# Interleaving two weight slots per row tile, an earlier square root for the key norms, and V transposes between the output gate's groups

## The chip, the cores and the metric

The kernel runs on one core of one Trainium2 chip. The metric is device time of one launch in microseconds (us). Before the change it is 1481.89 us, the median of three runs (1480.38 to 1483.07).

## What is computed

One inference step of a two-layer decoder, on 16 meta rows and 256 prompt rows of a new sequence and 8 new rows of each of 8 running sequences: 336 rows of 1024 columns, later 322 or 320, since some rows are needed no longer. Cut to what matters:

```python
def _swiglu(x, w_gu, w_down):
    gate, up = jnp.split(x @ w_gu, 2, axis=-1)
    return (jax.nn.silu(gate) * up) @ w_down

# layer 0 (RWKV-7 time mix), layer 1 (short convolution)
x = x + 0.5 * _swiglu(_rmsnorm(x, n_a), w_gu_a, w_down_a)
x = x + mixer(_rmsnorm(x, n_m))
x = x + 0.5 * _swiglu(_rmsnorm(x, n_b), w_gu_b, w_down_b)

# in the time mix, h is the normed x, xx the shifted h minus h
xr, xw, xk, xv, xa, xg = [h + xx * mu[c] for c in range(6)]
k = xk @ w_rkv[1]; v = xv @ w_rkv[2]
kk = k * k_k, divided by its norm in each head of 64
g = sigmoid(xg @ g1) @ g2
S = S * d + (S @ -kk) b + v k        # for each step in time; y = S @ r
out = ((groupnorm(y) + bonus) * g) @ w_o
```

A final RMSNorm ends the step; the states of the mixers are outputs too.

## The kernel before

Every matmul with weights is done with 32-bit values split in a high and a low part, in three passes: `(w_hi, x_hi)`, `(w_hi, x_lo)`, `(w_lo, x_hi)`. Activations lie transposed: 128 columns of the model on the partitions, 336 rows of the sequence along the free axis, so x is eight tiles, k = 0 to 7. A **slot** is 16 weight tiles of 128x128 (1 MB): two output tiles for all eight k, 48 matmuls of 336, 322 or 320 columns.

There are two slot buffers, even and odd. For every slot SyncE loads `w_raw`, ScalarE makes `w_hi` (L243, in `split_act`) when TensorE has used the slot before last, VectorE makes `w_lo` (L248, in `split_dve`), and TensorE waits for that (`lo_ready`, in `pe_slot_wait`). So from the end of one slot to the start of the slot two further on there lie one `w_hi`, one `w_lo`, and whatever stands ahead of them on ScalarE and VectorE. In a steady stretch the slot in between covers this.

The stages in order: FFN 0 (`ffn_pe`, `ffn_dve` with its inner `gu_slot`, ScalarE's side at L383 and L385; weights `in_gu`, then `in_down`), the time mix, the projection `wo`, FFN 1, FFN 2, the input projection of the convolution, the projection `scout`, FFN 3, the final norm. Each engine has its program written out by hand, and semaphores link them; so what stands behind a waiting instruction on its engine waits as well.

- An FFN's first slot (slot 0) runs while x_hi (L307) and x_lo (L295) arrive one tile at a time; TensorE waits for each tile (L330, in `pe_pair`). Slot 1 follows, the sum of squares (L311) stands between them. ScalarE first splits slot 2, then makes 1/rms by a logarithm and an exponential (`norm_act`, L315 and L317), VectorE scales the two results of slot 0 (L422, L423) and then makes `w_lo` of slot 2.
- The time mix begins with the key projection: slots 0 to 3 of `in_mix` with the mixed tiles x_hi (L1117) and x_lo (L1375), each slot run whole (L804). Later the sum of squares of every key head is turned into its inverse norm: VectorE's maximum, ScalarE's Sqrt (L1206), VectorE's reciprocal (L1437), TensorE's spreading over a head's partitions (L852). Sqrt stands between two of four groups of sigmoids on ScalarE (L1131).
- After the V projection TensorE runs the output gate as four groups of two output tiles (`lora_out`, L830), then turns V of the first two chunks (`turn_v`, L958; ScalarE copies the result to `uvs`, L1275), does the first `couple_v` (L967), then `state_rows` (L1032): 256 small matmuls that multiply the states of the eight running sequences with their rows. The chain over the chunks follows (from L983).
- `wo` and `scout` (`project_pe`, L498) take four slots from o_hi and o_lo. Slot 2 writes the PSUM banks of slot 0, so it waits for `x_new`: VectorE's L275, which adds a result to x, for both output tiles of slot 0. Between these two, VectorE's program has the split of slot 2.

Of the kernel before, what the change touches and what calls it, by code (L numbers as in the profile page):

```python
# [77 lines left out]
def build_program(nc, x_dram, vec_dram, const_dram, shift_dram, conv_dram, wkv_dram, gu_dram, down_dram,  # L78
                  mix_dram, wo_dram, scin_dram, scout_dram, blockeye_dram, y_out, wkvp_out, wkvs_out, shift_out,
                  convo_out, zt_dram, tt_dram):  # L80
    with ExitStack() as ctx:
# [330 lines left out]
        def ffn_dve(dve, f):  # L412
# [4 lines left out]
            def gu_slot(i, par, tiles, first=False):  # L417
                s = 2 * i + par
                if first:
                    norm_dve(dve, {0: 0, 1: 2, 2: 3, 3: 5}[f], n)  # L420
# [61 lines left out]
        def project_pe(pe, name, q, n, olo_base):  # L482

            first = stream[name][0]
            for s in range(4):
                pe_slot_wait(pe, first + s)
                pe.wait_ge(x_new, 8 * q + 2 * s - 2)
                if s == 0:
                    pe.wait_ge(scaled, SCALED_BEFORE[name])
                    if name == "wo":  # L490
                        pe.wait_ge(mix_evac, MIX_GROUPS - 4)
                banks = ((2 * s) % 4, (2 * s + 1) % 4)
                for k in range(KT):
                    if s == 0:
                        pe.wait_ge(olo_ready, olo_base + k + 1)
                    for j in range(2):
                        for i, (w, v) in enumerate(passes(whi[s % 2], wlo[s % 2], ohi, olo)):
                            last = pe.matmul(PS[:, banks[j], :n], w[:, (2 * k + j) * P:(2 * k + j + 1) * P], v[:, k, :n],  # L498
                                             start=(k == 0 and i == 0), stop=(k == KT - 1 and i == 2))
# [270 lines left out]
        def mix_pe(pe):  # L770
# [167 lines left out]
        def chain_pe(pe):  # L938
# [7 lines left out]
            def turn_v(i):  # L946
# [3 lines left out]
                else:  # L950
                    pe.wait_ge(vy_padded, 1)
                    pe.wait_ge(mix_evac, 21)
# [149 lines left out]
        def mix_act(act):  # L1102
# [140 lines left out]
            for s in range(4):  # L1243
                evac(GATE_GROUP + s, [(gate[:, m, :], ACT.Copy, None, False) for m in (2 * s, 2 * s + 1)])
            split(17)
            chain_act(act)
# [528 lines left out]
```

## Time and profile before

| | |
|---|---|
| median of three runs | 1481.89 us |
| profiled execution | 1481.93 us |
| its span, first to last instruction | 1480.1 us |
| TensorE busy | 1402.2 us, 95% |
| VectorE busy | 853.8 us, 58% |
| ScalarE busy | 584.7 us, 40% |
| mean granted TensorE clock | 0.965 |

The profiled execution is 0.04 us from the median. Times of rows are microseconds from the start of the span; a row of the timeline has start, duration, engine (PE is TensorE, PEld its weight load, DVE VectorE, ACT ScalarE, POOL GpSimd), line, operation, tiles, and in brackets how long the engine stood idle before it and what released it. TensorE's matmuls overlap: the distance of their starts tells the pace, not their durations. The granted clock is 1.00 at 2.4 GHz and 0.50 at 1.2 GHz.

### The profile page before, as it was taken

What the parts mean: (1) busy time and instruction counts of PE and PEld (TensorE: products, weight loads), DVE (VectorE), ACT (ScalarE), POOL (GpSimd) and SP (SyncE); (2) the same over time, 40 slices, a digit from 0 to 9 for tenths busy, and PEclk for the clock granted to TensorE, in tenths of its full rate; (3) what the DMA queues carried; (4) which work ended last, traced back from release to release, by engine and by line L of the source; (5) the groups of instructions that cost most, each with busy time, mean ns of one, the idle gap of its engine ahead of it and who ended that gap; (6) DMA issues with size and microseconds to landing.
All of it is one profiled execution on the core that took longest, in us unless ns stands there. A gap on an engine that the chain in (4) does not pass through costs nothing.

```text
span 1480.1 us, 28445 instructions
## 1 busy us (share of the span) xinstructions
PE 1402.2 (95%) x11742; PEld 1359.1 (92%) x11742; DVE 853.8 (58%) x1275; ACT 584.7 (40%) x754; POOL 22.8 (2%) x36
## 2 busy tenths in 40 slices
PE   4999999697799999899999999999999999999997
PEld 4999999586689996699999999999999999999997
DVE  4555544776868254665555455555546766555543
ACT  5333333476344331354333334433333235433332
POOL 0000000300000000200000000000000000000000
PEclk9999999898799797799999999999999999999999
DMA  4433334232135111034433444443444444434342
GB/s 193 151 140 138 137 131 155 86 116 85 60 84 187 36 48 53 29 131 154 142 142 126 147 162 150 154 142 124 139 157 149 147 143 140 167 143 142 128 155 96
DMA packets 44219, 188.97 MB, mean 128 GB/s; under 512 B 15888, under 2 KB 17296, under 8 KB 28016
## 3 DMA queue, kind: packets, MB, share of 16 engines
q1 hardware_dynamic: 44144, 187.89, 36.9%
q8 instruction: 57, 0.93, 0.3%
q14 instruction: 18, 0.15, 0.0%
HBM read 182.65 MB, written 5.22 MB: 127 GB/s over the span
## 4 chain that ended last, share of the span: by engine, by line
PE 87%; DVE 5%; ACT 4%; issue 2%; POOL 1%; DMA 1%; SPq 0%; ACTq 0%; DVEq 0%
PE psum L330 46%; PE psum L362 21%; PE psum L804 5%; PE psum L498 4%; ACT w_hi L243 2%; PE psum L1032 1%; DVE w_lo L248 1%; PE psum L983 1%; PE psum L1052 1%; PE psum L830 1%; PE psum L1001 1%; PE psum L958 1%; PE psum L876 1%; DMA w_raw<-in_gu 1%; PE psum L1048 1%
## 5 line engine op out<-in xcount | busy, mean ns | idle before, releaser
L330 PE MATMUL psum<-x_hi,w_hi 128*128 128x322 f32 (+2 forms) x1600 | 501.4, 313 | 23.5 <-DVE x_lo L295 17.8
L248 DVE TENSOR_TENSOR w_lo<-w_raw,w_hi 128x2048 fp32r<-128x2048 f32 (+1 forms) x188 | 388.2, 2065 | 226.3 <-ACT w_hi L243 225.9
L243 ACT ACTIVATE w_hi<-w_raw 128x2048 fp32r<-128x2048 f32 (+1 forms) x188 | 325.8, 1733 | 459.3 <-PE psum L330 227.2
L330 PE MATMUL psum<-x_lo,w_hi 128*128 128x322 f32 (+2 forms) x1600 | 500.8, 313 | 0.0
L330 PE MATMUL psum<-x_hi,w_lo 128*128 128x322 f32 (+2 forms) x1600 | 499.4, 312 | 0.0
L330 PEld LDWEIGHTS psum<-x_hi,w_hi 128*128 128x128 f32 x1600 | 302.2, 189 | 26.4 <-issue 22.7
L330 PEld LDWEIGHTS psum<-x_hi,w_lo 128*128 128x128 f32 x1600 | 302.9, 189 | 0.0
L330 PEld LDWEIGHTS psum<-x_lo,w_hi 128*128 128x128 f32 x1600 | 302.7, 189 | 0.3
L362 PE MATMUL psum<-h_hi,w_hi 128*128 128x322 f32 (+2 forms) x704 | 219.5, 312 | 0.0
L362 PE MATMUL psum<-h_lo,w_hi 128*128 128x322 f32 (+2 forms) x704 | 219.4, 312 | 0.0
L362 PE MATMUL psum<-h_hi,w_lo 128*128 128x322 f32 (+2 forms) x704 | 219.2, 311 | 0.0
L362 PEld LDWEIGHTS psum<-h_hi,w_hi 128*128 128x128 f32 x704 | 132.8, 189 | 0.0
L362 PEld LDWEIGHTS psum<-h_hi,w_lo 128*128 128x128 f32 x704 | 132.8, 189 | 0.0
L362 PEld LDWEIGHTS psum<-h_lo,w_hi 128*128 128x128 f32 x704 | 132.5, 188 | 0.0
L385 ACT ACTIVATE h_hi<-tmp 128x322 f32 (+5 forms) x88 | 41.9, 476 | 210.6 <-DVE tmp L427 210.6
L422 DVE TENSOR_TENSOR tmp<-psum,rstd 128x322 f32<-128x322 f32 (+2 forms) x88 | 43.7, 497 | 131.1 <-PE psum L330 106.7
L804 PE MATMUL psum<-x_hi,w_hi 128*128 128x336 f32 x208 | 70.0, 337 | 11.2 <-DVE x_lo L1375 11.2
L429 DVE TENSOR_TENSOR h_lo<-tmp,h_hi 128x322 f32 (+5 forms) x88 | 43.9, 498 | 63.8 <-ACT h_hi L385 63.8
L804 PE MATMUL psum<-x_lo,w_hi 128*128 128x336 f32 x208 | 68.5, 329 | 0.0
L804 PE MATMUL psum<-x_hi,w_lo 128*128 128x336 f32 x208 | 68.2, 328 | 0.0
L275 DVE SCALAR_TENSOR_TENSOR x<-psum,x 128x322 f32<-128x322 f32 (+5 forms) x48 | 23.7, 494 | 72.6 <-PE psum L362 62.4
L804 PEld LDWEIGHTS psum<-x_hi,w_hi 128*128 128x128 f32 x208 | 41.3, 198 | 16.1 <-issue 12.8
(200 smaller groups left out, 1394.2 us busy)
## 6 DMA issues: line engine op xcount, KB each, us to landing
w_raw<-in_gu SPq DMA_DIRECT2D x88, 1024.0 KB, 4.7
w_raw<-in_down SPq DMA_DIRECT2D x64, 704.0 KB, 4.1
w_raw<-in_mix SPq DMA_DIRECT2D x16, 1024.0 KB, 4.7
w_raw<-in_scin SPq DMA_DIRECT2D x12, 1024.0 KB, 4.8
w_raw<-in_wo SPq DMA_DIRECT2D x4, 1024.0 KB, 5.5
w_raw<-in_scout SPq DMA_DIRECT2D x4, 1024.0 KB, 4.7
s<-in_wkv SPq DMA_DIRECT2D x8, 256.0 KB, 3.4
out_wkvs<-s SPq DMA_DIRECT2D x8, 256.0 KB, 2.0
```

The source lines that it names most:

```text
L243: act.activation(whi[par][:, :tiles * P], raw[par][:, :tiles * P], ACT.Copy).then_inc(hi_ready, 1)
L248: dve.tensor_tensor(wlo[par][:, :n], raw[par][:, :n], whi[par][:, :n].bitcast(F32), ALU.subtract).then_inc(lo_ready, 1)
L275: dve.scalar_tensor_tensor(out=x[:, m, c:], in0=ps[:, :T - c], scalar=alpha, in1=x[:, m, c:], op0=ALU.mult, op1=ALU.add).then_inc(x_new, 1)
L330: last = pe.matmul(PS[:, banks[j], :n], w[:, (2 * k + j) * P:(2 * k + j + 1) * P], v[:, k, :n], start=(k == 0 and i == 0), stop=(k == KT - ...
L362: last = pe.matmul(PS[:, 4 + par, :n], w[:, k * P:(k + 1) * P], v[:, kk, :n], start=(kk == 0 and i == 0), stop=(kk == FT - 1 and i == 2))
L385: act.activation(hhi[:, bass.ds(s, 1), :n], tmp[3][:, :n], ACT.Copy).then_inc(hhi_ready, 1)
L422: dve.tensor_tensor(tmp[0][:, :n], PS[:, 2 * par, :n], rstd[:, :n], ALU.mult).then_inc(gate_scaled, 1)
L429: dve.tensor_tensor(hlo[:, bass.ds(s, 1), :n], tmp[3][:, :n], hhi[:, bass.ds(s, 1), :n].bitcast(F32), ALU.subtract).then_inc(hlo_ready, 1)
L498: last = pe.matmul(PS[:, banks[j], :n], w[:, (2 * k + j) * P:(2 * k + j + 1) * P], v[:, k, :n], start=(k == 0 and i == 0), stop=(k == KT - ...
L804: last = pe.matmul(PS[:, b + j, shift:shift + T], w[:, (2 * k + j) * P:(2 * k + j + 1) * P], v[:, k, :], start=(k == 0 and i == 0), stop=( ...
L830: last = pe.matmul(PS[:, b + j, shift:shift + T], w[:, tile * P:(tile + 1) * P], v[:, k, :], start=(n == 0 and i == 0), stop=(n == len(inn ...
L876: last = pe.matmul(PS[rows, 2 + c // 8, (c % 8) * HD:(c % 8 + 1) * HD], bk[rows, p, c, :, :].rearrange("p h t -> p (h t)"), con[rows, K_EY ...
```

## The change

Seven edits, by the lines of the new kernel where they are named so:

1. **FFN 0, front.** A generator `dual(lag)` yields tiles of slot 0 and slot 1 in turn, slot 1 `lag` tiles behind; `pe_tile` runs the six matmuls of one tile of one slot. FFN 0 uses a lag of 2; slot 0's last tile is then the 13th of 16 before the sum of squares (which now stands ahead of slot 1's last two tiles).
2. **`norm_act`.** Ahead of the wait for the sum of squares, for the time mix's norm and the final norm, one Ln of one column into a new tile `spare`.
3. **FFN `gu_slot` on VectorE.** For the first slot, the split of slot 2 stands ahead of the wait for 1/rms and of the scaling.
4. **Key projection.** Slots 0 and 1 in turn, with a lag of 3.
5. **Key norms.** VectorE's maximum and ScalarE's Sqrt stand before the first group of decay sigmoids, VectorE's reciprocal between the tiles of the receptance input.
6. **Output gate and V.** Gate group, `turn_v(0)`, two gate groups, `turn_v(1)`, gate group; the gate's PSUM banks change from (4, 6, 0, 2) to (4, 0, 2, 4), ScalarE's evacuations follow the same order, its split of the slot after (`split(17)`) goes behind them, and the semaphore values are fitted to it.
7. **`wo` and `scout`.** TensorE waits for both slots 0 and 1, then runs them in turn with a lag of 3; slots 2 and 3 as before.

```diff
+        def dual(lag):
+
+            for step in range(KT + lag):
+                if step < KT:
+                    yield 0, step
+                if step >= lag:
+                    yield 1, step - lag
...
-            gu_slot(0, 0, fresh=True)
-            norm_pe(pe, {0: 0, 1: 2, 2: 3, 3: 5}[f], 0, n)
-            gu_slot(0, 1)
+            if f == 0:
+                pe_slot_wait(pe, gu)
+                pe.wait_ge(scaled, d["scaled"] + 2)
+                for par, k in dual(2):
+                    if par == 0:
+                        pe.wait_ge(xlo_ready, 8 * d["ver"] + k + 1)
+                    elif k == 0:
+                        pe_slot_wait(pe, gu + 1)
+                    elif k == KT - 2:
+                        norm_pe(pe, 0, 0, n)
+                    last = pe_tile(pe, par, (2 * par, 2 * par + 1), k, n, xhi, xlo)
+                    if k == KT - 1:
+                        last.then_inc(slot_used, 1)
...
         def norm_act(act, norm, n):
+            if norm in (1, 6):
+                act.activation(spare[:, 0:1], con[:, K_ONES:K_ONES + 1], ACT.Ln)
...
                 if first:
+                    split_dve(dve, gu // 2 + i + 1, par, tiles)
                     norm_dve(dve, {0: 0, 1: 2, 2: 3, 3: 5}[f], n)
...
-                split_dve(dve, gu // 2 + i + 1, par, tiles)
+                if not first:
+                    split_dve(dve, gu // 2 + i + 1, par, tiles)
...
         def project_pe(pe, name, q, n, olo_base):
...
+            for s in range(2):
                 pe_slot_wait(pe, first + s)
                 pe.wait_ge(x_new, 8 * q + 2 * s - 2)
+            for s, k in dual(3):
                 if s == 0:
+                    pe.wait_ge(olo_ready, olo_base + k + 1)
+                last = pe_tile(pe, s, (2 * s, 2 * s + 1), k, n, ohi, olo)
...
-            for s in range(4):
-                project(s, XK, s == 0, s == 3, PAD)
+            pe_slot_wait(pe, MIXB)
+            banks = [open_group(), open_group()]
+            for par, k in dual(3):
...
+            for s in range(2, 4):
+                project(s, XK, False, s == 3, PAD)
...
+            act.wait_ge(kk_max, 1)
+            act.activation(tmp[3][0:HEADS, :T], tmp[3][0:HEADS, :T], ACT.Sqrt).then_inc(kk_root, 1)
             for s in range(4):
                 x_hi_tile(XR, 2 + s)
...
                 factors(s)
-                if s == 1:
-                    act.wait_ge(kk_max, 1)
-                    act.activation(tmp[3][0:HEADS, :T], tmp[3][0:HEADS, :T], ACT.Sqrt).then_inc(kk_root, 1)
...
                 low(XR, k)
                 if k == 1:
                     lora_low(1, 1)
...
+                if k == 3:
+                    dve.wait_ge(kk_root, 1)
+                    dve.reciprocal(rstd[0:HEADS, :], tmp[3][0:HEADS, :T]).then_inc(kk_inv, 1)
             split(6)
-            dve.wait_ge(kk_root, 1)
-            dve.reciprocal(rstd[0:HEADS, :], tmp[3][0:HEADS, :T]).then_inc(kk_inv, 1)
...
+            gate_group(0)
             turn_v(0)
+            gate_group(2)
+            gate_group(4)
             turn_v(1)
-            pe.wait_ge(mix_evac, 22)
+            gate_group(6)
+            pe.wait_ge(v_turned, 1)
+            pe.wait_ge(mix_evac, 21)
...
+            take_gate(0)
             take_v(0)
+            take_gate(1)
+            take_gate(2)
             take_v(1)
+            take_gate(3)
+            split(17)
```

How it moves instructions, at three places. First VectorE's program where FFN 0 begins its first pair of weight columns, right after the last x_lo (it reads the same in FFN 1 to 3). Before:

```order
L422 TENSOR_TENSOR tmp_62<-psum,rstd 128x336 [waits slot_used,rstd_ready]
L423 TENSOR_TENSOR tmp_64<-psum,rstd 128x336
L248 TENSOR_TENSOR w_lo_54<-w_raw_50,w_hi_52 128x2048 [waits hi_ready]
L427 TENSOR_TENSOR tmp_65<-tmp_63,tmp_64 128x336 [waits scaled,act_ready]
L429 TENSOR_TENSOR h_lo<-tmp_65,h_hi 128x336 [waits hhi_ready]
```

Now:

```order
L249 TENSOR_TENSOR w_lo_54<-w_raw_50,w_hi_52 128x2048 [waits hi_ready]
L455 TENSOR_TENSOR tmp_63<-psum,rstd 128x336 [waits slot_used,rstd_ready]
L456 TENSOR_TENSOR tmp_65<-psum,rstd 128x336
L461 TENSOR_TENSOR tmp_66<-tmp_64,tmp_65 128x336 [waits scaled,act_ready]
L463 TENSOR_TENSOR h_lo<-tmp_66,h_hi 128x336 [waits hhi_ready]
```

The split of slot 2 has moved ahead of the two scalings, and so ahead of their wait for `rstd_ready`.

Next TensorE's program in `scout`, around the fourth tile of slot 0 (`w_hi_52` and `w_lo_54` are the even buffer's, `w_hi_53` and `w_lo_55` the odd one's). Before:

```order
L498 MATMUL psum<-o_hi,w_hi_52 128x320 [waits olo_ready]
L498 MATMUL psum<-o_lo,w_hi_52 128x320
L498 MATMUL psum<-o_hi,w_lo_54 128x320
L498 MATMUL psum<-o_hi,w_hi_52 128x320
L498 MATMUL psum<-o_lo,w_hi_52 128x320
L498 MATMUL psum<-o_hi,w_lo_54 128x320
L498 MATMUL psum<-o_hi,w_hi_52 128x320 [waits olo_ready]
```

Now, in the same place:

```order
L349 MATMUL psum<-o_hi,w_lo_54 128x320
L349 MATMUL psum<-o_hi,w_hi_53 128x320
L349 MATMUL psum<-o_lo,w_hi_53 128x320
L349 MATMUL psum<-o_hi,w_lo_55 128x320
L349 MATMUL psum<-o_hi,w_hi_53 128x320
L349 MATMUL psum<-o_lo,w_hi_53 128x320
L349 MATMUL psum<-o_hi,w_lo_55 128x320
L349 MATMUL psum<-o_hi,w_hi_52 128x320 [waits olo_ready]
```

and at the end of slot 0, with the first row of slot 2 at the end:

```order
L349 MATMUL psum<-o_lo,w_hi_52 128x320
L349 MATMUL psum<-o_hi,w_lo_54 128x320
L349 MATMUL psum<-o_hi,w_hi_53 128x320
L349 MATMUL psum<-o_lo,w_hi_53 128x320
...
L349 MATMUL psum<-o_hi,w_lo_55 128x320
L349 MATMUL psum<-o_hi,w_hi_52 128x320 [waits x_new,lo_ready]
```

Before, the even buffer's slot ran on to its end and the odd one's 48 matmuls followed; now tiles take turns from the fourth on, and between slot 0's last matmul and slot 2's first there stand 24 matmuls. FFN 0 and the key projection have the same pattern, with lags of 2 and 3.

Last TensorE's program from the gate's groups to `state_rows`. Before:

```order
L830 MATMUL psum<-t_hi,w_lo_55 128x336
L958 MATMUL psum<-con,vy 64x64 [waits mix_evac,vy_padded]
L958 MATMUL psum<-con,vy 64x64 x15
L958 MATMUL psum<-con,vy 64x64 [waits v_turned]
L958 MATMUL psum<-con,vy 64x64 x15
L967 MATMUL psum<-uvs_102,z 32x64 [waits mix_evac]
L967 MATMUL psum<-uvs_102,z 32x64 x15
L1032 MATMUL psum<-ar,s_0_112 64x2x8 [waits mix_evac,s0_loaded0]
```

Now:

```order
L867 MATMUL psum<-t_hi,w_lo_55 128x336
L1005 MATMUL psum<-con,vy 64x64 [waits z_ready,mix_evac,vy_padded]
L1005 MATMUL psum<-con,vy 64x64 x15
L867 MATMUL psum<-t_hi,w_hi_53 128x336 [waits mix_evac]
...
L867 MATMUL psum<-t_hi,w_lo_55 128x336
L1005 MATMUL psum<-con,vy 64x64 [waits v_turned]
L1005 MATMUL psum<-con,vy 64x64 x15
L867 MATMUL psum<-t_hi,w_hi_53 128x336 [waits mix_evac]
...
L867 MATMUL psum<-t_hi,w_lo_55 128x336
L1014 MATMUL psum<-uvs_103,z 32x64 [waits mix_evac,v_turned]
L1014 MATMUL psum<-uvs_103,z 32x64 x15
L1079 MATMUL psum<-ar,s_0_113 64x2x8 [waits mix_evac,s0_loaded0]
```

The two turns (64x64 matmuls) stand between the gate's groups (`t_hi`, `t_lo`), the wait of the second turn for `v_turned` has 24 gate matmuls ahead of it, and 12 more stand between it and the first coupling.

## Rows read from the trace of the kernel before

**Rows 1.** The page, its busy engines and its chain by engine.

```profile
PE 1402.2 (95%) x11742; PEld 1359.1 (92%) x11742; DVE 853.8 (58%) x1275; ACT 584.7 (40%) x754; POOL 22.8 (2%) x36
...
PE 87%; DVE 5%; ACT 4%; issue 2%; POOL 1%; DMA 1%; SPq 0%; ACTq 0%; DVEq 0%
```

**Rows 2.** Windows: stretch, length, busy PE PEld DVE ACT POOL, granted clock, DMA, GB/s.

```profile
278.70:282.00 3.30, 3.21 (x11) 3.06 (x12) 3.30 (x6) 0.53 (x3) 3.30 (x7) 0.51 0.03 5
476.50:480.26 3.76, 3.75 (x64) 3.46 (x64) 1.80 (x1) 0.60 (x1) 0.00 (x0) 0.50 0.88 293
480.26:494.03 13.77, 13.77 (x258) 13.73 (x256) 0.00 (x0) 0.38 (x1) 0.00 (x0) 0.50 0.19 72
1207.50:1215.00 7.50, 7.50 (x52) 7.50 (x53) 3.97 (x6) 1.57 (x4) 0.00 (x0) 1.00 0.41 143
```

**Rows 3.** Timeline of FFN 0's front, from slot 0's end to slot 2's start.

```profile
28.37 1.92 ACT L243 ACTIVATE w_hi<-w_raw 128x2048 fp32r<-128x2048 f32 x1 [1.89 <-PE psum L330]
...
30.31 1.28 ACT L315 ACT_TABLE_LOAD   x1
...
33.36 0.49 ACT L317 ACTIVATE rstd<-ms 128x336 f32<-128x336 f32 x1
...
34.31 0.50 DVE L423 TENSOR_TENSOR tmp<-psum,rstd 128x336 f32<-128x336 f32 x1
...
34.72 2.28 DVE L248 TENSOR_TENSOR w_lo<-w_raw,w_hi 128x2048 fp32r<-128x2048 f32 x1
...
37.15 0.42 PE L330 MATMUL psum<-x_hi,w_hi 128*128 128x336 f32 x1 [0.87 <-DVE w_lo L248]
```

**Rows 4.** Timeline where slot 2 starts in FFN 1, FFN 2 and FFN 3.

```profile
657.92 0.41 PE L330 MATMUL psum<-x_hi,w_hi 128*128 128x322 f32 x1 [1.04 <-DVE w_lo L248]
...
895.90 0.41 PE L330 MATMUL psum<-x_hi,w_hi 128*128 128x322 f32 x1 [1.12 <-DVE w_lo L248]
...
1251.50 0.40 PE L330 MATMUL psum<-x_hi,w_hi 128*128 128x320 f32 x1 [1.03 <-DVE w_lo L248]
```

**Rows 5.** Timeline of the key projection: tiles arriving, slot 0's end.

```profile
284.30 0.42 PE L804 MATMUL psum<-x_hi,w_hi 128*128 128x336 f32 x1 [0.68 <-DVE x_lo L1375]
...
291.02 1.92 ACT L243 ACTIVATE w_hi<-w_raw 128x2048 fp32r<-128x2048 f32 x1 [2.16 <-PE psum L804]
```

**Rows 6.** Timeline around the square root of the key norms.

```profile
329.18 0.42 PE L830 MATMUL psum<-t_hi,w_hi 128*128 128x336 f32 x1 [1.86 <-ACT sw L1131]
...
340.41 1.28 ACT L1206 ACT_TABLE_LOAD   x1
341.70 0.48 ACT L1206 ACTIVATE tmp<-tmp 16x336 f32<-16x336 f32 x1
342.20 1.28 ACT L1131 ACT_TABLE_LOAD   x1
342.22 2.24 DVE L1437 RECIPROCAL rstd<-tmp 16x336 f32<-16x336 f32 x1 [2.98 <-ACT tmp L1206]
```

**Rows 7.** Timeline from the gate's last group to the first coupling.

```profile
467.99 0.77 ACT L1131 ACTIVATE vy<-psum 128x336 f32<-128x336 f32 x2
...
473.28 1.15 PE L958 MATMUL psum<-con,vy 64*64 64x64 f32 x32
...
475.86 0.60 ACT L1275 ACTIVATE uvs<-psum 128x512 f32<-128x512 f32 x1
...
476.51 1.98 PE L958 MATMUL psum<-con,vy 64*64 64x64 f32 x32 [2.09 <-ACT uvs L1275]
```

**Rows 8.** Timeline of `scout`: its start, and slot 0's end.

```profile
1207.40 0.38 PE L498 MATMUL psum<-o_hi,w_hi 128*128 128x320 f32 x1 [1.31 <-DVE tmp L573]
...
1208.13 2.29 DVE L248 TENSOR_TENSOR w_lo<-w_raw,w_hi 128x2048 fp32r<-128x2048 f32 x1
...
1214.69 0.49 DVE L275 SCALAR_TENSOR_TENSOR x<-psum,x 128x320 f32<-128x320 f32 x1 [3.47 <-PE psum L498]
...
1219.55 0.48 DVE L275 SCALAR_TENSOR_TENSOR x<-psum,x 128x320 f32<-128x320 f32 x1
```

More of the change, by code:

```diff
@@ L332, in pe_pair, with pe_tile @@
             last.then_inc(out_sem, 1)
+        def dual(lag):
[4 more added lines that the diff above has]
+                    yield 1, step - lag
+        def pe_tile(pe, par, banks, k, n, xh, xl, shift=0):
+            for j in range(2):
+                for i, (w, v) in enumerate(passes(whi[par], wlo[par], xh, xl)):
+                    last = pe.matmul(PS[:, banks[j], shift:shift + n], w[:, (2 * k + j) * P:(2 * k + j + 1) * P], v[:, k, :n],
+                                     start=(k == 0 and i == 0), stop=(k == KT - 1 and i == 2))
+            return last
         def ffn_pe(pe, f):
@@ L484, in project_pe @@
             first = stream[name][0]
-            for s in range(4):
+            pe.wait_ge(scaled, SCALED_BEFORE[name])
+            if name == "wo":
+                pe.wait_ge(mix_evac, MIX_GROUPS - 4)
+            for s in range(2):
                 pe_slot_wait(pe, first + s)
                 pe.wait_ge(x_new, 8 * q + 2 * s - 2)
+            for s, k in dual(3):
                 if s == 0:
-                    pe.wait_ge(scaled, SCALED_BEFORE[name])
-                    if name == "wo":
-                        pe.wait_ge(mix_evac, MIX_GROUPS - 4)
+                    pe.wait_ge(olo_ready, olo_base + k + 1)
+                last = pe_tile(pe, s, (2 * s, 2 * s + 1), k, n, ohi, olo)
+                if k == KT - 1:
+                    last.then_inc(slot_used, 1)
+            for s in range(2, 4):
+                pe_slot_wait(pe, first + s)
+                pe.wait_ge(x_new, 8 * q + 2 * s - 2)
                 banks = ((2 * s) % 4, (2 * s + 1) % 4)
                 for k in range(KT):
[L494 to L499, printed above, removed]
+                    last = pe_tile(pe, s % 2, banks, k, n, ohi, olo)
                 last.then_inc(slot_used, 1)
@@ L614, in build_program @@
         BANKS.update({V_GROUP + i: b for i, b in enumerate((0, 2, 0, 2))})
-        BANKS.update({GATE_GROUP + i: b for i, b in enumerate((4, 6, 0, 2))})
+        BANKS.update({GATE_GROUP + i: b for i, b in enumerate((4, 0, 2, 4))})
         Z_BANKS = (4, 6)
@@ L820, in lora_inner, with lora_out @@
                 last.then_inc(mix_out, 1)
-            def lora_out(slot, first_tile, inner, shift=0):
-                for m in range(0, KT, 2):
+            def lora_out(slot, first_tile, inner, shift=0, tiles=(0, KT)):
+                for m in range(*tiles, 2):
                     b = open_group()
@@ L832, in lora_out @@
                     last.then_inc(mix_out, 1)
-            for s in range(4):
-                project(s, XK, s == 0, s == 3, PAD)
+            pe_slot_wait(pe, MIXB)
+            banks = [open_group(), open_group()]
+            for par, k in dual(3):
+                if par == 0:
+                    pe.wait_ge(xlo_ready, 8 * XK + k + 1)
+                elif k == 0:
+                    pe_slot_wait(pe, MIXB + 1)
+                last = pe_tile(pe, par, (banks[par], banks[par] + 1), k, T, xhi, xlo, PAD)
+                if k == KT - 1:
+                    last.then_inc(mix_out, 1)
+            for s in range(2, 4):
+                project(s, XK, False, s == 3, PAD)
             lora_inner(4, XW)
@@ L905, in mix_pe @@
             pe.wait_ge(lora_lo, 4)
-            lora_out(15, 0, (0, 1))
-            chain_pe(pe)
+            chain_pe(pe, lambda m: lora_out(15, 0, (0, 1), tiles=(m, m + 2)))
             pe.wait_ge(y_evac, CHUNKS)
@@ L951, in turn_v @@
                     pe.wait_ge(vy_padded, 1)
[L952 removed]
+                    pe.wait_ge(mix_evac, 19)
+                    pe.wait_ge(z_ready, 16)
                 for p in range(PAIRS):
@@ L1242, in mix_act @@
                 evac(V_GROUP + s, [(vy[:, m, PAD:], ACT.Copy, None, False) for m in (2 * s, 2 * s + 1)])
[L1243 to L1246, printed above, removed]
+            chain_act(act, lambda s: evac(GATE_GROUP + s, [(gate[:, m, :], ACT.Copy, None, False) for m in (2 * s, 2 * s + 1)]),
+                      split)
             for p in range(PAIRS):
@@ L1259, in mix_act, with chain_act @@
             project_act(act, "wo", 2)
-        def chain_act(act):
+        def chain_act(act, take_gate, split):
             def take_v(i):
```

23 lines of the change are left out of this document (14 added, 9 removed).

## The prediction

> **What bounds the kernel now.** I began with the page's busy times and its chain [rows 1]: TensorE is busy for 95% of the span and holds 87% of the chain. An edit can only save time where TensorE stands still or runs at half clock, and it costs time wherever it makes TensorE wait. So I looked next in the timeline for TensorE's waits at each place that the change touches [rows 3 to 8], and in windows for its clock [rows 2]. A full-size slot is 48 matmuls; in `scout` 52 matmuls take 7.50 us at full clock [rows 2], 0.146 us each, so about 7.0 us a slot and 0.88 us for six of them, one tile of one slot.
>
> The clock matters as much as the waits. After 9.46 us without matmuls the key projection starts at a granted 0.51 for 3.3 us [rows 2]; after a wait of 2.09 us [rows 7] the turn of V, the coupling and all of `state_rows` run at 0.50, the latter 258 matmuls in 13.77 us [rows 2], 53 ns each. Waits of 0.87 to 1.31 us [rows 3, 4, 8] stand in dense stretches at full clock; `scout` after its wait of 1.31 us shows 1.00 [rows 2].
>
> Everything is reckoned against the profiled execution, 1481.93 us, of which 1480.1 us are span; the median of the runs, 1481.89 us, is 0.04 us from it, so one sum serves for both.
>
> **FFN 0, front: +1.5 us of delay and +1.6 us of clock.** Here slots 0 and 1 are not starved: x_lo comes fast enough, and slot 1 covers the work that follows slot 0's end. That work is w_hi at 28.37, a table load at 30.31, the logarithm, another load, the exponential till 33.85, two scalings till 34.81 and w_lo till 37.00; slot 2 starts at 37.15 and waits just 0.87 us [rows 3]. Taking turns moves slot 0's end back by about four tiles of slot 1: before it lies 4 times six matmuls later, 4 × 0.92 = 3.7 us, to about 32.1. From slot 0's end to the second scaling's end it is 34.81 − 28.37 = 6.44 us, which gives 38.5; the split is no longer behind it, as edit 3 puts it ahead of the norm. Slot 2 then starts at 38.6 instead of 37.15: +1.5. TensorE, done with both slots near 35.1, stands still for 3.5 us instead of 0.87. That is longer than the 2.09 us after which the clock was at half [rows 7], so I take the half-clock stretch seen after the key projection's long wait, 3.3 us at 0.51 [rows 2], which loses half its length, 1.6. The bounds are 0 (as after 1.31 us) and 2.5.
>
> **The early Ln: 0.** Before the time mix and at the end it brings a table load forward that ScalarE already does while it waits for other work; at 1.28 us for such a load [rows 3] it could at most save or cost that once. Both places have a w_hi or another wait ahead of them, so I take neither.
>
> **The split ahead of the scaling: −3.6 us.** In FFN 1 to 3 TensorE waits for w_lo of slot 2: 1.04, 1.12 and 1.03 us [rows 4]. That split (2.28 us, [rows 3]) stood behind the scaling, which stood behind 1/rms, while VectorE was idle. Now it is done before 1/rms is there. What is late next is `scaled` itself, for slot 2 reuses the banks; in FFN 0's rows the second scaling ends at 34.81, 2.3 us before slot 2 starts [rows 3], so it doesn't hold slot 2 back. The record of the last matmul reaches 0.16 us past where the next would begin, hence 3 × 1.2 = 3.6 at most; the low bound is 3.2, the waits alone.
>
> **Key projection: −1.0 us.** Tiles arrive every 1.9 us, and TensorE waits 0.68 us for one of them [rows 5], twice so, and 0.36 once. With two slots per tile this time is filled, but slot 0 ends later: 292.8 instead of 291.0 [rows 5]. Slot 2 needs w_hi (1.92 us) and w_lo (2.29 us) after that, so 297.2; it came at 298.2. The gain is 1.0, not the 1.9 that slots 0 and 1 gain. Bounds 0 and −1.9.
>
> **Key norms: −0.85 us.** At 340.41 ScalarE loads a table for the Sqrt, takes 0.48 us for it and loads the sigmoid's table again [rows 6]: 3.04 us. Ahead of the first sigmoids one load and the Sqrt remain, 1.76 us, in front of the decay's sigmoids for which TensorE already waits 1.86 us [rows 6]. Net ScalarE gains 1.28 us. The reciprocal (2.24 us, [rows 6]) now sits in the middle of VectorE's low halves of the next input and gives part back. Between 0 and −1.3 I take −0.85; ScalarE, then VectorE, lead here, TensorE doesn't.
>
> **V between the gate's groups: −2.6 us and −4.3 us of clock.** TensorE ends the gate at 473.28, turns V(0), then waits 2.09 us for ScalarE's copy, which had w_hi ahead of it [rows 7]; from 476.51 on all is at half clock, and `state_rows` begins at 480.26 [rows 2, 7]. In the new order turn 0 first waits for the last V evacuation, which ends at 468.76 [rows 7], for about 1.0 us; the gate's groups (1.85 us each) cover the copy, and the second turn, the fourth group and the coupling end near 477.7: 2.6 earlier. The wait of 2.09 us is gone and 1.0 is below the 1.31 that didn't lower the clock [rows 8], so `state_rows` should begin at full clock. Its 256 small matmuls, which were at half throughout, would take 6.9 us instead of 13.8 if they stayed there. I don't think they do, since at half clock they ran to their end without its coming back [rows 2]; between 0 and −6.9 I take some 60%, −4.3.
>
> A rule in the Trainium skill, "TensorE: Matmul & The Clock Gate", section "A second HAM failure mode: psum-queue depth-cycling", speaks against this: many small idles between groups of matmuls make the clock fall and rise too. By it the fall at 476.5 needn't come from the one wait, and the sum would lack these 4.3. The rows before [rows 2, 7] show the fall with the wait and can't part the two.
>
> **`wo` and `scout`: +2.1 and +2.1, and in `scout` +3.05 and +1.6.** Neither waits for tiles after its first [rows 8], so taking turns fills nothing. Slot 2 needs both results of slot 0 added to x: from the first L275 to the end of the second it is 1220.03 − 1214.69 = 5.34 us [rows 8], VectorE's split of slot 2 lying between. Before, slot 1's 7.0 us covered this. Now 24 matmuls do, 24 × 0.146 = 3.5 us; with 0.2 of hand-over TensorE waits 2.1 us in each. In `scout` TensorE moreover started slot 0 at 1207.40 while slot 1's w_lo was still to come, from 1208.13 till 1210.42 [rows 8]. Now it waits for it: start at 1210.45, +3.05. The wait grows from 1.31 to 4.4 us, which I price like FFN 0's with 1.6 (bounds 0 and 2.5).
>
> **The sum.** 1.5 + 1.6 + 0 − 3.6 − 1.0 − 0.85 − 2.6 − 4.3 + 2.1 + 2.1 + 3.05 + 1.6 = −0.4. So 1481.9 − 0.4 = 1481.5 us: gains and losses of some 12 us cancel. A difference under 0.2% (3.0 us) can't be told from none here.
>
> **Rivals.**
> 1. *Faster, the clock is kind.* `state_rows` stays at full clock to its end (another −2.6), or neither long wait lowers the clock (−3.2), or both: 1478.9, 1478.3 or 1475.7. For it: 1.31 us of waiting lowered nothing [rows 8]. Against: 9.46 us did, and 2.09 may have. Chance 0.20.
> 2. *Slower, the clock is lost before `state_rows`.* By the mechanism of small idles (the page named above): a stop of 1.0 us, two turns of 64-row matmuls and the coupling come close together, and the clock is at half before the state rows begin; then only the 2.6 is left. 1481.5 + 4.3 = 1485.8. It decides if the clock reads 0.50 at the first state row. Chance 0.17.
> 3. *Slower, the new 2.1 us waits in `wo` and `scout` lower the clock as the 2.09 us one did* [rows 7]: each 1.6 more, 1484.7. Against: they stand in dense stretches of wide matmuls. Chance 0.12.
> 4. *The interleaving doesn't delay slot 2,* as the work behind slot 0 is faster than I reckon: without 2.1, 2.1 and 3.1, 1474.2. The rows give each link a duration, so 0.06.
>
> My own sum has 0.45. Faster than 1478.9: most of 1 and 4, 0.22. Slower than 1484.9: most of 2, half of 3 and errors of my own sum, 0.23. The rest, 0.55, is within 0.2%. From 1477.5 to 1486.5 the range takes in the single cases of 1, 2 and 3, and leaves out 4 and pairs. The likeliest case alone spans 1479.5 to 1483.5, from the bounds of the key norms, the key projection and the clock.
>
> **What would show it.** In the new profile: slot 2 of FFN 1 to 3 without a wait; in FFN 0 a wait of some 3.5 us before slot 2; in `wo` and `scout` waits of about 2 us before slot 2, released by L275's line; `scout`'s first matmul right after slot 1's w_lo; the key projection's slot 2 one us earlier; the first state row near 3 us earlier against the gate's start, with the clock at 1.00 for part of them. If `scout`'s first matmul comes before slot 1's w_lo, or slot 2 of `wo` starts without a wait, the forecast's losses are wrong; if the state rows read 0.50 throughout, its largest gain is.

## The result, and the profile after

The changed kernel takes 1487.53 us, the median of seven runs (1485.86 to 1489.46); the kernel before, run beside it, 1481.78 us (1478.19 to 1483.18, seven runs). The ratio is 1.0036, with a 95% interval of 1.0023 to 1.0049: 5.3 us slower, beyond 0.2%. 1481.5 was forecast, with a range up to 1486.5. The profiled execution took 1489.46 us, the longest of the seven, 7.5 us over the profiled execution of before; what the stages below add up to is thus some 2 us more than the medians show.

The page of the changed kernel, its busy engines and its chain:

```profile
PE 1406.2 (95%) x11742; PEld 1363.0 (92%) x11742; DVE 853.9 (57%) x1275; ACT 583.4 (39%) x755; POOL 22.8 (2%) x36
...
PE 88%; DVE 5%; ACT 4%; issue 2%; DMA 1%; POOL 0%; SPq 0%; ACTq 0%; DVEq 0%
```

TensorE is still the bound. With as many matmuls it is busy 4.0 us longer than in [rows 1], at a mean granted clock of 0.961 instead of 0.965: it ran slower for longer, and did not only wait. The timeline of the changed kernel at the places of the prediction (answering to [rows 3], [rows 5], [rows 8] and, for `wo`, to the same lines there):

```profile
32.28 1.92 ACT L244 ACTIVATE w_hi<-w_raw 128x2048 fp32r<-128x2048 f32 x1 [6.10 <-PE psum L349]
...
38.76 0.42 PE L333 MATMUL psum<-x_hi,w_hi 128*128 128x336 f32 x1 [3.24 <-DVE tmp L456]
...
295.37 1.92 ACT L244 ACTIVATE w_hi<-w_raw 128x2048 fp32r<-128x2048 f32 x1 [4.10 <-PE psum L349]
...
299.67 0.42 PE L841 MATMUL psum<-x_hi,w_hi 128*128 128x336 f32 x1 [0.69 <-DVE w_lo L249]
...
621.32 0.49 DVE L276 SCALAR_TENSOR_TENSOR x<-psum,x 128x322 f32<-128x322 f32 x1 [9.28 <-PE psum L349]
...
626.20 0.49 DVE L276 SCALAR_TENSOR_TENSOR x<-psum,x 128x322 f32<-128x322 f32 x1
...
626.83 0.39 PE L349 MATMUL psum<-o_hi,w_hi 128*128 128x322 f32 x1 [1.97 <-DVE x L276]
...
1205.60 2.29 DVE L249 TENSOR_TENSOR w_lo<-w_raw,w_hi 128x2048 fp32r<-128x2048 f32 x1
...
1208.25 0.60 PE L349 MATMUL psum<-o_hi,w_hi 128*128 128x320 f32 x1 [4.70 <-DVE w_lo L249]
...
1227.35 0.39 PE L349 MATMUL psum<-o_hi,w_hi 128*128 128x320 f32 x1 [2.00 <-DVE x L276]
```

The new waits stand where they were forecast, at nearly their size: 3.24 us before FFN 0's slot 2 (released by the second scaling), 1.97 and 2.00 us before slot 2 of `wo` and `scout` (released by the second L276), 4.70 us before `scout`'s first matmul. Before slot 2 of FFN 1 to 3 no wait is left. The clock is another matter. Windows of the changed kernel, with the columns of [rows 2]:

```profile
38.80:40.20 1.40, 1.40 (x9) 1.40 (x10) 0.51 (x1) 0.81 (x3) 0.00 (x0) 1.00 1.02 433
40.30:43.60 3.30, 3.30 (x13) 3.30 (x12) 2.50 (x4) 2.48 (x3) 0.00 (x0) 0.50 0.15 62
478.30:480.50 2.20, 2.20 (x79) 2.20 (x77) 0.52 (x1) 1.64 (x1) 0.00 (x0) 1.00 0.85 260
480.60:490.00 9.40, 9.40 (x182) 9.40 (x180) 1.67 (x1) 0.39 (x1) 0.00 (x0) 0.50 0.32 115
627.40:630.70 3.30, 3.30 (x14) 3.30 (x14) 2.79 (x5) 2.74 (x4) 0.00 (x0) 0.50 0.69 285
1208.30:1214.40 6.10, 6.10 (x23) 6.10 (x24) 0.39 (x1) 0.00 (x0) 0.00 (x0) 0.50 0.52 172
1228.10:1231.40 3.30, 3.30 (x14) 3.30 (x13) 2.78 (x5) 2.55 (x4) 0.00 (x0) 0.50 0.66 276
```

The clock is at half for 3.3 us after the waits of 1.97 and 2.00 us too, for 6.1 us after `scout`'s, and in the state rows from 2.2 us after their start on. Stage by stage, from the starts of the same `w_hi` and matmuls in both traces (after minus before, and how much each stage added):

| up to | difference | added | forecast |
|---|---|---|---|
| end of FFN 0 | +2.3 | +2.3 | +3.1 |
| end of the key projection | +1.5 | −0.8 | −1.0 |
| pairs of heads, after the key norms | +0.5 | −1.0 | −0.85 |
| start of `wo` (610.41, now 607.64) | −2.8 | −3.3 | −6.9 |
| end of `wo` | +0.9 | +3.7 | +2.1 |
| start of `scout`'s front | −2.5 | −3.4 | −2.4 |
| end of `scout` | +7.5 | +10.0 | +6.75 |
| end | +7.6 | +0.1 | −1.2 |

### The profile page after: what moved, and what is told of

Its sections match the earlier page's. It is cut to its first block, busy times and chain, and to the rows that moved or that the text cites. A ratio compares the mean times of both kernels' runs of the same rounds, so it can differ in the third digit from the quotient of the medians.

```text
span 1487.7 us, 28446 instructions
## 1 busy us (share of the span) xinstructions
PE 1406.2 (95%) x11742; PEld 1363.0 (92%) x11742; DVE 853.9 (57%) x1275; ACT 583.4 (39%) x755; POOL 22.8 (2%) x36
## 4 chain that ended last, share of the span: by engine, by line
PE 88%; DVE 5%; ACT 4%; issue 2%; DMA 1%; POOL 0%; SPq 0%; ACTq 0%; DVEq 0%
PE psum L333 47%; PE psum L394 21%; PE psum L349 6%; PE psum L841 4%; ACT w_hi L244 2%; DVE w_lo L249 1%; PE psum L1079 1%; PE psum L1030 1%; PE psum L1099 1%; PE psum L1048 1%; PE psum L1005 1%; PE psum L923 1%; PE psum L1095 1%; PE psum L1063 1%; DMA w_raw<-in_gu 1%
## 5 line engine op out<-in xcount | busy, mean ns | idle before, releaser
L333 PE MATMUL psum<-x_hi,w_hi 128*128 128x322 f32 (+2 forms) x1568 | 488.9, 312 | 4.8 <-DVE tmp L456 3.2
L333 PE MATMUL psum<-x_hi,w_lo 128*128 128x322 f32 (+2 forms) x1568 | 490.0, 312 | 0.0
L333 PE MATMUL psum<-x_lo,w_hi 128*128 128x322 f32 (+2 forms) x1568 | 489.5, 312 | 0.0
L333 PEld LDWEIGHTS psum<-x_hi,w_hi 128*128 128x128 f32 x1568 | 297.5, 190 | 6.3 <-DVE tmp L456 3.5
L333 PEld LDWEIGHTS psum<-x_hi,w_lo 128*128 128x128 f32 x1568 | 296.2, 189 | 0.0
L333 PEld LDWEIGHTS psum<-x_lo,w_hi 128*128 128x128 f32 x1568 | 295.3, 188 | 0.2
L276 DVE SCALAR_TENSOR_TENSOR x<-psum,x 128x322 f32<-128x322 f32 (+5 forms) x48 | 23.7, 494 | 87.6 <-PE psum L394 62.3
L841 PE MATMUL psum<-x_hi,w_hi 128*128 128x336 f32 x176 | 58.0, 329 | 0.7 <-DVE w_lo L249 0.7
L841 PE MATMUL psum<-x_lo,w_hi 128*128 128x336 f32 x176 | 57.2, 325 | 0.0
L841 PE MATMUL psum<-x_hi,w_lo 128*128 128x336 f32 x176 | 56.9, 324 | 0.0
L349 PE MATMUL psum<-o_hi,w_hi 128*128 128x322 f32 (+1 forms) x128 | 43.9, 343 | 8.7 <-DVE w_lo L249 4.7
```

Source lines behind the costliest of these rows:

```text
L276: dve.scalar_tensor_tensor(out=x[:, m, c:], in0=ps[:, :T - c], scalar=alpha, in1=x[:, m, c:], op0=ALU.mult, op1=ALU.add).then_inc(x_new, 1)
L349: last = pe.matmul(PS[:, banks[j], shift:shift + n], w[:, (2 * k + j) * P:(2 * k + j + 1) * P], v[:, k, :n], start=(k == 0 and i == 0), st ...
L841: last = pe.matmul(PS[:, b + j, shift:shift + T], w[:, (2 * k + j) * P:(2 * k + j + 1) * P], v[:, k, :], start=(k == 0 and i == 0), stop=( ...
```

## The experiments

All are timed in five rounds with the kernel before on the same chip; the ratios are to that. The changed kernel was not timed again beside them, and the kernel before has medians from 1479.98 to 1482.45 us beside them; so ratios are compared where they and the medians differ. T is the theory that each new wait of TensorE brings a half-clock stretch besides its own length, and that the state rows lose the clock by themselves; in the runs of part 3 and of parts 4 and 5 it stands for what the traces gave for these parts.

**Without part 7.** `project_pe` as it was:

```diff
-            for s, k in dual(3):
+            for s in range(4):
...
```

> wo and scout run their four slots one after the other again; everything else of the change stays. Theory T (each wait of 2.0 us before slot 2 in wo and scout brings a half-clock stretch of its own, and scout's late start one of about 6 us): the edit cost 3.7 us in wo and 10.1 us in scout by the two traces, so 1487.5 - 13.8 = 1473.7 us, and no fall of the clock between 616 us and the end of FFN 3. Rival R (the edit costs only the delays, as forecast with 8.85 us, and the clock falls there for another reason): 1478.7 us, with half-clock stretches left in the projections.

Measured: 1473.40 us, ratio 0.9963 (0.9946 to 0.9980). The median is T's number (1473.7), but the kernel before, timed beside it, was 1.8 us faster than beside the changed kernel; by the ratio the gain is 5.5 us (3.0 to 8.0), with T's 8.1 and the rival's 3.1 both at the interval's ends. So the time doesn't decide; the trace does. The window of this run from `wo` to the end of FFN 3:

```profile
608.00:1464.00 856.00, 849.03 (x5713) 846.69 (x5711) 489.30 (x650) 334.73 (x369) 1.97 (x2) 1.00 0.41 141
```

A granted 1.00 throughout: the half-clock stretches around slot 2 and in `scout` belong to part 7. (Before this window, `wo` begins with 2.9 us at half clock; it does so for 6.0 us in the kernel before and in the changed one.) And `scout` adds 0.1 us to the difference from the kernel before in this trace, where the changed kernel's adds 10.0.

**Without parts 1 and 7.** FFN 0's two slots run whole again, too:

```diff
-            if f == 0:
-                pe_slot_wait(pe, gu)
...
+            gu_slot(0, 0, fresh=True)
+            norm_pe(pe, {0: 0, 1: 2, 2: 3, 3: 5}[f], 0, n)
+            gu_slot(0, 1)
```

> As the run before, and FFN 0 too runs slot 0 and slot 1 one after the other. By the traces FFN 0's front cost 2.3 us, and with the split ahead of the scaling its slot 2 should start without the old wait of 0.87 us as well: T: 1473.7 - 2.3 - 0.9 = 1470.5 us. If the interleaving in FFN 0 cost nothing (rival), the time equals that of the run before.

Measured: 1470.68 us, 0.9937 (0.9915 to 0.9959). T's number again, but the interval overlaps that of the run before, so that the time alone doesn't show what FFN 0's interleaving cost. In the two traces FFN 0 ends 1.3 us behind the kernel before with it and 2.3 us ahead without it: 3.6 us, against 2.7 by the medians.

**The waits before slot 2 filled with matmuls.**

```diff
             for s in range(2, 4):
+                if s == 2:
+                    for _ in range(13):
+                        pe.matmul(PS[:, 7, :n], ohi[:, 0, :P], ohi[:, 1, :n], start=True, stop=True)
                 pe_slot_wait(pe, first + s)
```

> The changed kernel with 13 idle matmuls on o_hi into an unused PSUM bank between slot 1 and the wait for slot 2 in wo and scout; they fill about 1.9 us of the 2.0 us wait and their results are not used. T: slot 2 starts as late as in the changed kernel but at full clock, so 1.6 us less in each: 1487.5 - 3.2 = 1484.3 us. Rival R: the clock falls as before, 1487.5 us, or later by what the fill delays.

Measured: 1482.93 us, 1.0026 (1.0012 to 1.0040): 4.6 us under the changed kernel by the medians, but only 1.5 by the ratios (1.0036 before), whose intervals overlap. The runs scatter from 1481.5 to 1487.2. The time alone doesn't part T from its rival. What the run was made for is seen in its windows:

```profile
624.00:630.70 6.70, 6.65 (x45) 6.42 (x44) 6.03 (x10) 3.48 (x6) 0.00 (x0) 1.00 0.43 159
1222.00:1228.00 6.00, 5.91 (x41) 5.68 (x40) 5.32 (x10) 3.33 (x6) 0.00 (x0) 1.00 0.52 172
1206.80:1210.90 4.10, 4.10 (x16) 4.10 (x17) 0.35 (x1) 0.00 (x0) 0.00 (x0) 0.50 0.73 256
```

Slot 2 of `wo` starts at 626.84, as late as in the changed kernel, but the clock stays at 1.00 around slot 2 of both projections; it falls where nothing was filled, at `scout`'s start. So the wait's length and the half clock after it are two prices, and the idle TensorE is what causes the second.

**Slot 2 with banks of its own.**

```diff
-                pe.wait_ge(x_new, 8 * q + 2 * s - 2)
-                banks = ((2 * s) % 4, (2 * s + 1) % 4)
+                if s == 3:
+                    pe.wait_ge(x_new, 8 * q + 2 * s - 2)
+                banks = (4, 5) if s == 2 else (2, 3)
...
```

> The changed kernel with PSUM banks 4 and 5 for slot 2 of wo and scout, so that it waits for w_lo only and not for x_new. T: slot 0's end to w_lo is some 4.3 us, of which slot 1's rest covers 3.5, so a wait of 0.8 us instead of 2.0 and no fall of the clock: 1.2 + 1.6 = 2.8 us less in each, 1487.5 - 5.6 = 1481.9 us. If x_new is not what holds slot 2 (rival), 1487.5 us.

Measured: 1481.43 us, 1.0010 (0.9994 to 1.0027). T's time as a ratio, 1.0001, lies in the interval, the rival's 1.0036 doesn't. The timeline shows the shorter wait with its new releaser, and the window over it the clock:

```profile
622.38 0.42 PE L349 MATMUL psum<-o_hi,w_hi 128*128 128x322 f32 x1 [0.84 <-DVE w_lo L249]
...
1219.34 0.42 PE L349 MATMUL psum<-o_hi,w_hi 128*128 128x320 f32 x1 [0.87 <-DVE w_lo L249]
```

```profile
618.00:630.00 12.00, 11.15 (x73) 10.64 (x72) 10.14 (x16) 6.39 (x9) 0.00 (x0) 1.00 0.30 95
1216.00:1228.00 12.00, 11.06 (x74) 10.57 (x74) 10.18 (x17) 6.48 (x11) 0.00 (x0) 1.00 0.36 116
```

**Part 7 alone on the kernel before.**

```diff
-            for s in range(4):
+            for s, k in dual(3):
...
```

> The kernel before with part 7 alone, slots 0 and 1 of wo and scout in turn. If the parts add up (T): 1481.8 + 13.8 = 1495.6 us. If part of the loss in wo and scout belongs to other parts (rival, as where the earlier chain changes how wo begins): by the forecast's own terms 1481.8 + 8.9 = 1490.7 us.

Measured: 1494.47 us, 1.0084 (1.0064 to 1.0104), 13.7 us by the medians and 12.4 by the ratio (9.5 to 15.4): T's 13.8 lies inside, the rival's 8.9 just outside. Both slot 2 waits, 1.96 and 2.02 us here, are followed by a half clock again. Part 7's loss is its own and adds up.

**Part 6 alone on the kernel before.**

```diff
-            turn_v(0)
-            turn_v(1)
+            gate_group(0)
+            turn_v(0)
+            gate_group(2)
+            gate_group(4)
+            turn_v(1)
+            gate_group(6)
...
```

> The kernel before with part 6 alone, the turns of V between the gate's groups. By the two traces the first state row starts 2.3 us earlier against the gate's start, the state rows take 9.6 to 12.0 us in the runs so far instead of 13.6, and about 3 us of it reach the chain's end: theory T (the clock is lost inside the state rows themselves, wherever the wait before them went): 1481.8 - 3.1 = 1478.7 us, with the first state row at a granted clock of 1.00 and the last at 0.50. Rival F (the forecast: the old wait of 2.09 us was what lost the clock, and 4.3 us come back): 1474.9 us.

Measured: 1478.39 us, 0.9985 (0.9973 to 0.9996); T's 1478.7, and not the rival's 1474.9. The windows of the state rows:

```profile
478.20:483.10 4.90, 4.90 (x170) 4.90 (x171) 2.29 (x1) 1.99 (x2) 0.00 (x0) 1.00 0.33 116
483.20:487.60 4.40, 4.40 (x89) 4.40 (x86) 0.00 (x0) 0.00 (x0) 0.00 (x0) 0.50 0.61 235
```

They begin at 1.00, 29 ns a matmul, and go on at 0.50, 49 ns. In the eight traces with part 6 and nothing else among the state rows the fall comes 2.0 to 5.0 us after the first state row, with no wait close before it. What in these rows lowers the clock is not shown.

**The old wait filled, on the kernel before.**

```diff
             turn_v(0)
+            for _ in range(11):
+                pe.matmul(PS[:, 7, :T], thi[:, 0, :P], thi[:, 1, :], start=True, stop=True)
             turn_v(1)
```

> The kernel before with 11 matmuls of 128x336 on t_hi into an unused PSUM bank between the two turns of V, where TensorE waited 2.09 us; their results are not used. If that wait lowered the clock (forecast), turn 1 and the coupling now run at full clock, the clock falls only inside the state rows, 2 to 5 us after their start as in the runs with part 6, and the state rows take 9.6 to 12.0 us instead of 13.6: 1481.8 - 1.8 - 1.6 to 4.0 = 1476.0 to 1478.4 us. If the narrow matmuls of the turns and the coupling lower it (rival), it falls before the first state row again: 1481.8 us.

Measured: 1482.15 us, 0.9994 (0.9982 to 1.0007). The time is the rival's, but the trace is as forecast:

```profile
475.49:477.58 2.09, 2.09 (x65) 1.93 (x65) 1.79 (x1) 0.60 (x1) 0.00 (x0) 1.00 0.96 331
477.60:482.10 4.50, 4.50 (x158) 4.50 (x156) 0.00 (x0) 0.38 (x1) 0.00 (x0) 1.00 0.83 292
482.20:488.90 6.70, 5.66 (x104) 5.54 (x102) 0.00 (x0) 0.00 (x0) 0.00 (x0) 0.50 0.02 7
```

The second turn and the coupling, all at 0.50 in [rows 2], run at 1.00 once the wait before them is filled; the fall comes inside the state rows, 4.6 us after the first. So the narrow matmuls of the turns and the coupling don't have to lower the clock. That the wait did it at 476.5 fits, but this trace doesn't prove it, for in the trace of part 3 alone (below) the same wait stands unfilled and the clock holds as well:

```profile
474.69 1.15 PE L960 MATMUL psum<-con,vy 64*64 64x64 f32 x32 [2.09 <-ACT uvs L1277]
```

```profile
474.69:476.70 2.01, 2.01 (x64) 1.93 (x64) 1.79 (x1) 0.60 (x1) 0.00 (x0) 1.00 1.02 312
476.78:480.30 3.52, 3.52 (x124) 3.52 (x122) 0.00 (x0) 0.00 (x0) 0.00 (x0) 1.00 0.92 318
480.45:487.00 6.55, 6.02 (x115) 5.92 (x114) 0.00 (x0) 0.38 (x1) 0.00 (x0) 0.50 0.13 48
```

Of the four traces with this wait, the clock falls at it in three (the kernel before, part 7 alone, parts 4 and 5) and only inside the state rows in this one. So the wait of 2.09 us doesn't lower the clock in every execution, and where it doesn't, the state rows do. Back to the run with the wait filled: its third window also has a stop of 1.0 us, most likely because the second half of the states was not loaded yet. This trace is 1.0 us ahead of the kernel before already at the gate's start; at the first chain step it is 5.1 us ahead, at the last one 2.2 us, and where `wo` starts 1.1 us. The steps of the chain in between wait on each other across engines and vary from one execution to the next. What was won ahead of them arrived only in part, and in the median not at all; why the chain gave it back stays open.

**Wide matmuls among the state rows.**

```diff
+                        if q == 3 and hh == 1:
+                            pe.matmul(PS[:, 7, :T], thi[:, 0, :P], thi[:, 1, :], start=True, stop=True)
```

> Parts 2 to 6 with one wide matmul of 128x336 on t_hi into an unused PSUM bank after every 16 of the 256 state-row matmuls, 16 in all; their results are not used. T (the narrow state rows themselves lose the clock): with wide matmuls among them the clock stays, 256 x 27 ns + 16 x 0.15 us = 9.3 us instead of about 11.8, and the steps after them begin at full clock: 1470.7 - 2.5 to 3.5 = 1467.2 to 1468.2 us. Rival (the clock falls from the stops around the turns of V, before the state rows): the added matmuls only cost, 16 x 0.15 to 0.28 = 2.4 to 4.5 us: 1473.1 to 1475.2 us.

Measured: 1482.63 us, 1.0012 (0.9999 to 1.0026), 11 us by the ratios over the same kernel without them: far outside both expectations. Its windows:

```profile
474.80:477.00 2.20, 2.20 (x50) 1.82 (x48) 0.54 (x1) 1.63 (x1) 0.00 (x0) 1.00 0.83 256
477.10:497.00 19.90, 19.90 (x223) 15.64 (x222) 1.65 (x1) 0.38 (x1) 0.00 (x0) 0.50 0.15 54
```

The clock fell 2.3 us in all the same, and each wide matmul cost far more than its 0.15 us, as the timeline shows while the clock was still full:

```profile
474.77 0.64 PE L1062 MATMUL psum<-ar,s 64*64 64x16 f32 x16
475.35 0.42 PE L1066 MATMUL psum<-t_hi 128*128 128x336 f32 x1
475.70 0.64 PE L1062 MATMUL psum<-ar,s 64*64 64x16 f32 x16
```

From one group of 16 state rows to the next it is 0.93 us, where the state rows alone take 16 × 29 ns = 0.46 us. This run doesn't test what it was made for.

**Part 3 alone; parts 4 and 5 alone.**

```diff
                 if first:
+                    split_dve(dve, gu // 2 + i + 1, par, tiles)
                     norm_dve(dve, {0: 0, 1: 2, 2: 3, 3: 5}[f], n)
...
```

> The kernel before with part 3 alone, in all four FFNs (FFN 0's slots one after the other). T: the waits before slot 2 go, 4 x 1.2 = 4.8 us: 1481.8 - 4.8 = 1477.0 us. In the runs with part 3 so far FFN 0's slots also came 7.386 us apart instead of 7.440; if that comes from part 3, it shows here, and if it comes from another part (the tile added by part 2 moves the tiles behind it), it doesn't.

> The kernel before with parts 4 and 5 alone. T: the two traces give -0.9 for the key projection and -0.95 for the key norms, 1481.8 - 1.85 = 1479.9 us. Rival (one of them only moves the wait, and the next stage takes it back): 1480.9 us or more.

Measured: part 3 1475.29 us, 0.9966 (0.9952 to 0.9981), a gain of 5.0 by the ratio for the 4.8 expected. Parts 4 and 5 1482.11 us, 1.0000 (0.9985 to 1.0015), with runs from 1474.4 to 1484.4: no gain is seen, which is nearer the rival, but the interval still holds T's 1.85 us. Its trace is 1.9 us ahead up to 391 us of the kernel before, as expected; then the clock was at half for longer. The same 94 matmuls, in the kernel before:

```profile
403.86:408.90 5.04, 5.04 (x94) 4.27 (x96) 2.19 (x5) 0.82 (x3) 0.00 (x0) 0.66 0.23 36
```

and with parts 4 and 5:

```profile
401.95:408.15 6.20, 6.20 (x94) 5.04 (x96) 2.20 (x5) 1.19 (x3) 0.00 (x0) 0.52 0.21 32
```

In this stretch 1.2 us went, and the rest, with 1.3 more, in the chain. Whether that happens in most executions one trace can't tell.

**Towards a better version.** Parts 2 to 6 and the same reordering in the convolution, and this once more without the early Ln:

```diff
                 if s == 0:
+                    split_dve(dve, first // 2 + 1, 0, BIG)
                     norm_dve(dve, 4, n)
...
```

> Parts 2 to 6, and the split of slot 2 ahead of the wait for 1/rms in the convolution's input projection as well, as part 3 does in the FFNs. That place has the same wait before slot 2, so 1.2 us less than parts 2 to 6 alone (1470.7): 1469.5 us, and no wait there. If the split there is not what slot 2 waits for (rival), 1470.7 us.

> Parts 3 to 6 with the convolution's split ahead too, but without part 2, the early Ln and its tile. Forecast's term, 0: as with part 2, 1469.1 us. Rival (the early table load saves 1.28 us at the two places): 1471.7 us. If the closer slots of FFN 0 come from the tile that part 2 adds, they are 7.440 us apart again and FFN 0 takes 1.0 us longer.

Measured: 1469.14 us, 0.9921 (0.9905 to 0.9938), the fastest of all and 11.7 us under the kernel before by the ratio; without the Ln and its tile 1470.97 us, 0.9931 (0.9915 to 0.9946). The two intervals overlap, and both overlap that of parts 2 to 6 alone. In the traces the convolution's wait of 1.56 us before slot 2 is gone and that stage is 1.8 us shorter than in the kernel before; the times alone don't show it.

## Why the prediction was wrong

- **`wo` and `scout`, the step that failed most.** The delays were right: 2.1 was forecast for each slot 2 and 1.97 and 2.00 came, 3.05 for `scout`'s start and the wait grew by 3.4. The failing step was to give the two waits of 2 us no clock price: rival 3, with 0.12, was what happened, 1.6 each, and the run with the waits filled shows it. And `scout`'s long wait was priced like FFN 0's with 1.6 (bounds 0 and 2.5), yet its half clock lasted 6.1 us in this trace and in part 7's alone, worth 3.05; in the runs with filled waits and with banks of their own it lasted 4.2 and 3.4 us after a wait as long. So this price isn't fixed. Together 13.7 instead of 8.85.
- **V between the gate's groups.** The first state row came 2.3 us earlier (forecast 2.6), and at full clock. The term that was mis-sized is the clock's, 4.3: of 13.6 us the state rows kept 11.7 in the profiled execution and 9.4 to 12.0 in others, and of what they gained only part came through the chain. Part 6 alone is worth 2.4 by the medians, not 6.9. Rival 2 had its number nearly right by another way: the clock wasn't lost before the state rows but in them. The Trainium skill's rule of small idles ("TensorE: Matmul & The Clock Gate", "A second HAM failure mode: psum-queue depth-cycling") isn't borne out here: with the one long wait filled, the second turn and the coupling ran at 1.00, and in the trace of part 3 alone they did so with the wait unfilled. That trace also goes against the prediction's own premise, that the wait of 2.09 us is what puts the state rows at half clock.
- **FFN 0.** Slot 2 at 38.76 against the forecast 38.6, the half-clock stretch 3.3 us as taken: right, the first in part by luck. Slot 0's last tile has five tiles of slot 1 ahead of it, not four, worth 4.6 us by the prediction's own price. Its end moved by 3.9 only, as slot 0 began 0.3 us earlier in this execution and lost the delays that its last tiles had before (their starts stood 1.18 and 1.36 us apart, not 0.92). That only 2.3 of 3.1 are left at FFN 0's end has a cause that wasn't forecast, below.
- **The split ahead of the scaling** was right: 1.3, 1.4 and 1.2 us in FFN 1 to 3, and in its run alone 5.0 with FFN 0's own.
- **Key projection and key norms**: 0.8 and 1.0 against 1.0 and 0.85, right as delays in this trace; alone they gave no measurable time, so that they are worth 1.85 in the median is not shown.
- **The early Ln** at 0: with and without it the intervals overlap.

As a sum, −0.4 missed +4.9 in the projections and +3.6 around V; what FFN 0 to 3 gave otherwise changes the rest by less than 1 us in this trace. Nearly all of the first was a price of the clock, and of the second about 2.5 us; 1.0 of it was given back in the chain. The prediction had the two waits and the loss around V as rivals, but at 0.12 and 0.17, and its range held only one of them at a time; the longer half clock in `scout` stood in none.

## What to carry to other kernels

A wait of TensorE can have two prices, its length and the half-clock stretch after it. Here waits of 2.0 us in the midst of dense matmuls cost 1.6 us more (four of four), those of 4.7 us 1.7 to 3 us more, and waits of 0.8 to 1.3 us none. Between the turns of V one of 2.09 us lowered the clock at once in three traces of four. So ask of each new wait near 2 us whether the clock will fall after it, and book that as a range. Taking two weight slots in turn paid here, if at all, only where tiles arrive slower than TensorE uses them (0.8 us in the key projection); elsewhere it moved both slots' ends together and uncovered the work between a slot's end and the next slot of its buffer. A gain ahead of a chain that runs across engines shouldn't be booked in full at its end.

## What the runs showed that was not expected

The pace of TensorE changed with part 2, a tile of 8 columns and one small instruction. Between 60 and 180 us of FFN 0, the kernel before, then the best version, which has part 2's `spare` tile, then the same without part 2:

```profile
60.00:180.00 120.00, 120.00 (x776) 120.00 (x775) 66.94 (x82) 45.26 (x49) 0.00 (x0) 1.00 0.39 137
```

```profile
60.00:180.00 120.00, 120.00 (x781) 120.00 (x781) 68.29 (x82) 44.40 (x51) 0.00 (x0) 1.00 0.39 134
```

```profile
60.00:180.00 120.00, 120.00 (x776) 120.00 (x775) 67.33 (x81) 44.53 (x50) 0.00 (x0) 1.00 0.38 134
```

781 matmuls instead of 776 in the same 120 us, at the same clock. All seven variants with the tile have FFN 0's slots 7.386 us apart, all without it 7.440, whatever else they change; it saves 1.0 us there. In the changed kernel the pace also gains 0.4 us in each of FFN 1 and FFN 2, and loses 0.2 in FFN 0's second half and 1.1 in FFN 3, so that little is left of it in the sum. The early Ln itself isn't run before FFN 0's end; so the tile's place in memory or the changed program may do it, which wasn't tried.
